# Diffusion backbone on one core: first eight modulation blocks in seven slots, sums of squares between them, x times the inverse ahead

## Chip, cores and metric

One core of one Trainium2 chip (trn2). The metric is device time in microseconds of one execution; a kernel's time is the median of its runs, and one further execution was profiled.

## The reference, cut to what matters

Two layers of a diffusion backbone act on 256 latent and 256 context tokens of width 1024. Every sub-layer is an RMSNorm, a shift and scale that come from a conditioning vector through one large matrix product per layer (the modulation), the sub-layer itself, and a gated addition. The change lies in the first norm of layer 0 and what stands around it.

```python
def rmsnorm(x, gain):
    xf = x.astype(jnp.float32)
    y = xf * lax.rsqrt(jnp.mean(xf * xf, axis=-1, keepdims=True) + EPS)
    return (y * gain.astype(jnp.float32)).astype(x.dtype)

def ada_mod(cond, w, b):
    m = jax.nn.silu(cond) @ w + b
    return jnp.split(m[..., None, :], 6, axis=-1)
...
        sh_m, sc_m, g_m, sh_f, sc_f, g_f = ada_mod(c, w_ada[layer], b_ada[layer])
        h = modulate(rmsnorm(x, norm_mix[layer]), sh_m, sc_m)      # h * (1 + scale) + shift
        y = even_mixer(h, w_in_even[j], ...)                       # begins with h @ w_in, 1024 x 1536
```

Behind it come the mixer, a dense SwiGLU, and in layer 1 a gated linear recurrence and top-2-of-8 experts, whose weights are most of the 480 MB that are read.

## The kernel before

**Precision.** Every large product is taken from fp32 in three passes of a high and a low part, both in fp32r (`three`, L633 to L638). The high part is made by ScalarE (L1533 for weights, L1583 for the first h), the low part by VectorE as the difference (L1919, L1975).

**Weights.** A projection's weights come in units of 128 x 1024 (512 KB), six raw slots (`raw`), each split into `w_hi` and `w_lo`; unit u waits for the split of unit u - 6 (`lo_done`). All loads are issued by SP in one order written out by hand (from L506 for modulation blocks, L469 for units), and a wait on SP holds everything that stands behind it.

**Modulation.** w_ada of a layer is taken in three thirds of 2048 columns, each in eight blocks of 128 rows (1 MB). Block a = 8t + kt belongs to third t. TensorE multiplies it with the conditioning vectors in `ada_unit` (L650, four fp32 matmuls of 512 columns, shown as eight instructions) and counts `ada_used`. There are three slots: two in the arena, one in `scratch`. The places in the arena for blocks 8 to 23 are columns 6144 and 8192. When eight blocks are done, ScalarE copies the row out (L1605), TensorE picks it into columns (`ada_pick`, L666), and VectorE adds the bias (`ada_cols`) and forms the coefficients.

**The beginning.** SP loads the small vectors, constants, x and ctx (each two tiles of 512 KB) and modulation blocks 0 to 2; blocks 3 to 7 each wait until their slot is used up. TensorE transposes x and ctx into eight tiles xT (L687), multiplies blocks 0 and 1, then makes eight sums of squares with a matrix of ones (`norm_sum`, L674), then blocks 2 to 7. The squares (L1550) alternate between two places, so each waits for the sum two ahead. VectorE scales the sum (L1960), ScalarE takes the Sqrt (L1577), VectorE the reciprocal (L1962). When the coefficients stand, `norm_dve` on VectorE takes, for each of the eight tiles, x times the inverse (L1985), two modulations of 256 columns (L1988), and the low part of the tile two back (L1975), with ScalarE's high part (L1583) between; four temporary tiles lie at arena columns 7680 to 9727, on the later places of modulation blocks. Therefore block 9 and 10 wait on SP for `h_done` 8 (L498).

**The first projection.** Its first two blocks of columns have four units each; a unit has 24 matmuls. Behind each unit stands one modulation block: blocks 8 to 11 in the first, 12 to 15 in the second. Ahead of block 8 SP issues the masks (448 KB), the DFT constants (640 KB), gmlp_w and gmlp_b (256 KB each), then block 8, unit 6, block 9, unit 7 and so on. GpSimd copies the masks once.

**Later.** The same pattern of units and modulation blocks goes on through layer 0. The expert weights run through a ring of 14 slots (L585), each freed by a split or by a use.

Of the kernel before, what the change touches and what calls it, by code (L numbers as in the profile page):

```python
# [34 lines left out]
D = 1024  # L35
# [23 lines left out]
R = 6  # L59
# [47 lines left out]
VEC_ROWS, B_ROWS = 12544, 12672  # L107
STATS = 13056
# [127 lines left out]
def build(nc, x, c, ctx_in, c_ctx, w_ada, b_ada, norm_mix, norm_ffn, norm_out, w_in_even, gmlp_wt, gmlp_b,  # L236
# [3 lines left out]
    with es:  # L240
# [3 lines left out]
        def sem(name):  # L244
            return es.enter_context(nc.semaphore(name))
# [50 lines left out]
        def ar(at, n):  # L296
            return arena[:, at:at + n]
# [27 lines left out]
        ada_in = [sem(f"ada_in{k}") for k in range(A_SLOTS)]  # L325
        ada_used, ada_half, ada_red = sem("ada_used"), sem("ada_half"), sem("ada_red")
# [60 lines left out]
        def ada_slot(a):  # L387

            at = A_SLOT_AT[a // KT]
            return scratch[:, :] if ada_place(a) == A_ACC else ar(at[ada_place(a)], A_COLS)  # L390
# [7 lines left out]
        def moe_seen(n):  # L398

            k = n % M_RING  # L400
            earlier = len(range(k, U_MOE, R)) if k < R else 0
            return moe_in[k], 16 * (earlier + n // M_RING + 1)
# [60 lines left out]
        def _(sp):  # L463
# [17 lines left out]
            def ada_load(a):  # L481

                t, kt = a // KT, a % KT
                last = max((b for b in range(a) if ada_place(b) == ada_place(a)), default=None)
                if a == 10:
                    sp.wait_ge(ada_used, 8)
                elif last is not None and last < A_PE:

                    sp.wait_ge(ada_used, last + 1)
                elif last is not None and ada_place(a) == A_ACC:  # L490

                    sp.wait_ge(ada_used, A_PE + 1)
# [12 lines left out]
                src = w_ada[t // 3][kt * P:(kt + 1) * P, t % 3 * A_COLS:(t % 3 + 1) * A_COLS]  # L505
                sp.dma_start(ada_slot(a), src).then_inc(ada_in[ada_place(a)], 16)  # L506
# [126 lines left out]
        def _(pe):  # L633
# [884 lines left out]
        def _(act):  # L1518
# [34 lines left out]
            def norm(n, width, layer, sh, streams):  # L1553


                act.wait_ge(coef_rdy, n)
# [18 lines left out]
            def norm_std(n, width):  # L1575
                act.wait_ge(var_done, n + 1)
                act.activation(ar(NORM_AT[n] + 2 * NT, width), ar(NORM_AT[n] + 2 * NT, width),  # L1577
                               ACT.Sqrt).then_inc(std_done, 1)

            def norm_hi(n, width):  # L1580
# [25 lines left out]
            norm_hi(0, NT)  # L1606
# [298 lines left out]
        def _(dve):  # L1905
# [50 lines left out]
            def norm_var(n, width):  # L1956

                inv = ar(NORM_AT[n] + 2 * NT, width)
                dve.wait_ge(sq_mm, KT * (n + 1))
                dve.tensor_scalar(inv, ps[:, 3, 0:width], 1.0 / D, EPS, ALU.mult, ALU.add).then_inc(var_done, 1)  # L1960
                dve.wait_ge(std_done, n + 1)
                link(dve.reciprocal(inv, inv))  # L1962

            def norm_dve(n, width, layer, gain, sh, sc, streams):

                base = NORM_AT[n]
                inv = ar(base + 2 * NT, width)
                for s in range(2):
                    m = dve.scalar_tensor_tensor(coef[:, :, s], adaT[:, layer, sc * KT:(sc + 1) * KT, s], 1.0,
                                                 vT[:, gain + layer * KT:gain + (layer + 1) * KT], ALU.add, ALU.mult)  # L1970
                link(m)

                def lo_h(kt):
                    dve.wait_ge(hhi_done, KT * n + kt + 1)
                    dve.tensor_tensor(hl(kt, 0, width), ar(base + (3 + kt % 4) * NT, width),  # L1975
                                      hh(kt, 0, width).bitcast(F32), ALU.subtract).then_inc(h_done, 1)

                for kt in range(KT):
                    if kt >= 2:
                        lo_h(kt - 2)  # L1980
                    if kt >= 4:

                        dve.wait_ge(h_done, KT * n + kt - 3)
                    t = ar(base + (3 + kt % 4) * NT, width)
                    link(dve.tensor_tensor(t, xT[:, kt, 0:width], inv, ALU.mult))  # L1985
                    for s in range(streams):
                        a, b = s * N_LAT, (s + 1) * N_LAT
                        m = dve.tensor_scalar(t[:, a:b], t[:, a:b], coef[:, kt, s:s + 1],  # L1988
                                              adaT[:, layer, sh * KT + kt, s:s + 1], ALU.mult, ALU.add)
                    m.then_inc(h32_done, 1)  # L1990
                    if n == 0 and kt in (6, 7):
                        split_to(split[0] + 1)
                lo_h(KT - 2)
                lo_h(KT - 1)

# [669 lines left out]
```

## Time and profile before

| | us |
|---|---|
| median of 3 runs | 1907.58 |
| lowest, highest | 1905.51, 1910.87 |
| the profiled execution: its own time | 1913.76 |
| its span, first to last instruction | 1911.9 |
| PE busy | 1767.9 (92%) |
| PEld busy | 1318.7 (69%) |
| DVE busy | 847.0 (44%) |
| ACT busy | 684.1 (36%) |
| chain that ended last | PE 69%, DMA 15%, DVE 7%, ACT 4%, SPq 3%, issue 2% |
| HBM read | 477.03 MB |
| mean granted TensorE clock | 0.966 |

PE is TensorE's matmul, PEld its weight load, DVE VectorE, ACT ScalarE, SP the engine whose queue issues the loads. The clock is a share of full speed, 2.4 GHz; the lower level is 0.50, 1.2 GHz. A matmul's end is modelled, so in a row of several the step from start to start is the better measure. An "idle before" in brackets names what ended it.

### The profile page before, as it was taken

The numbers are of one execution on the slowest core, as the hardware profiler recorded it, in microseconds if no ns is written. First come the engines' busy times: TensorE is split into PE (matmuls) and PEld (weight loads), VectorE is DVE, ScalarE is ACT, GpSimd is POOL, SyncE is SP. The second block draws the span as 40 slices with busy tenths as digits, with TensorE's granted clock in tenths as the row PEclk, the third lists the DMA queues.
The fourth block names the chain that finished last, engine by engine and source line by source line (L and its number), as shares of the span: only waits on it lengthen the run. The fifth ranks groups of instructions, "written<-read, shape, count | busy, mean of one in ns | idle before, by whom it ended". The sixth has DMA issues, their size and how long they took to land.

```text
span 1911.9 us, 28155 instructions
## 1 busy us (share of the span) xinstructions
PE 1767.9 (92%) x11488; PEld 1318.7 (69%) x11488; DVE 847.0 (44%) x1197; ACT 684.1 (36%) x893; POOL 3.5 (0%) x6
## 2 busy tenths in 40 slices
PE   5899899999998988997889999999998899998988
PEld 2567677888886978887777887766546777763434
DVE  2524424434533555656549965554104444520011
ACT  3222521222225535444358754443003444400001
POOL 0000000000000000000000000000000000000000
PEclk8899999999999999998979999999999899999998
DMA  8654166433631322120149979999999999999995
GB/s 324 246 186 154 34 231 231 172 103 138 225 98 46 100 89 77 60 84 23 67 166 322 377 297 407 409 409 409 408 409 385 340 359 381 401 409 409 409 409 238
DMA packets 161843, 479.96 MB, mean 251 GB/s; under 512 B 14976, under 2 KB 58160, under 8 KB 155568
## 3 DMA queue, kind: packets, MB, share of 16 engines
q1 hardware_dynamic: 161712, 478.14, 66.4%
q8 instruction: 91, 1.49, 0.3%
q14 instruction: 40, 0.33, 0.0%
HBM read 477.03 MB, written 1.05 MB: 250 GB/s over the span
## 4 chain that ended last, share of the span: by engine, by line
PE 69%; DMA 15%; DVE 7%; ACT 4%; SPq 3%; issue 2%; DVEq 0%; ACTq 0%
PE ps L636 15%; PE ps L638 15%; PE ps L637 15%; DMA arena<-in_moe_up 6%; DMA raw<-in_moe_up 5%; PE ps L1369 4%; DMA arena<-in_moe_w 3%; PE ps L1440 3%; SPq L585 2%; DVE w_lo L1919 2%; PE ps L1358 2%; PE ps L650 2%; PE ps L1432 1%; PE ps L1190 1%; ACT w_hi L1533 1%
## 5 line engine op out<-in xcount | busy, mean ns | idle before, releaser
L1919 DVE TENSOR_TENSOR w_lo<-raw,w_hi 128x1024 fp32r<-128x1024 f32 x242 | 292.5, 1221 | 367.8 <-ACT w_hi L1533 365.5
L1533 ACT ACTIVATE w_hi<-raw 128x1024 fp32r<-128x1024 f32 x242 | 252.5, 1056 | 463.2 <-PE ps L638 350.2
L636 PE MATMUL ps<-h_hi,w_hi 128*128 128x512 f32 (+1 forms) x736 | 284.2, 386 | 15.6 <-DVE h_lo L2013 10.8
L637 PE MATMUL ps<-h_hi,w_lo 128*128 128x512 f32 (+1 forms) x736 | 277.3, 377 | 0.0
L638 PE MATMUL ps<-h_lo,w_hi 128*128 128x512 f32 (+1 forms) x736 | 277.1, 376 | 0.0
L1919 DVE TENSOR_TENSOR w_lo<-arena,w_hi 128x1024 fp32r<-128x1024 f32 x144 | 172.0, 1220 | 123.8 <-ACT w_hi L1533 121.0
L1533 ACT ACTIVATE w_hi<-arena 128x1024 fp32r<-128x1024 f32 x144 | 151.4, 1059 | 160.4 <-DMA arena<-in_moe_up 92.0
L636 PEld LDWEIGHTS ps<-h_hi,w_hi 128*128 128x128 f32 x736 | 142.3, 193 | 59.6 <-issue 35.2
L638 PEld LDWEIGHTS ps<-h_lo,w_hi 128*128 128x128 f32 x736 | 141.6, 192 | 25.3
L637 PEld LDWEIGHTS ps<-h_hi,w_lo 128*128 128x128 f32 x736 | 142.2, 193 | 23.7 <-issue 0.5
L1369 PE MATMUL ps<-arena 128*64 128x256 f32 x1024 | 128.9, 387 | 9.5 <-DMA arena<-in_moe_up 7.8
L636 PE MATMUL ps<-w_hi,s_hi 128*128 128x512 f32 x336 | 134.8, 401 | 2.7 <-DVE s_lo L2442 2.4
L637 PE MATMUL ps<-w_hi,s_lo 128*128 128x512 f32 x336 | 131.6, 392 | 0.0
L638 PE MATMUL ps<-w_lo,s_hi 128*128 128x512 f32 x336 | 131.6, 392 | 0.0
L636 PE MATMUL ps<-w_hi,h_hi 128*128 128x512 f32 (+1 forms) x328 | 117.3, 358 | 0.0
L638 PE MATMUL ps<-w_lo,h_hi 128*128 128x512 f32 (+1 forms) x328 | 114.9, 350 | 0.0
L637 PE MATMUL ps<-w_hi,h_lo 128*128 128x512 f32 (+1 forms) x328 | 114.8, 350 | 0.0
L1369 PEld LDWEIGHTS ps<-arena 128*64 128x64 f32 x1024 | 66.7, 136 | 64.1 <-DMA arena<-in_moe_up 28.8
L1369 PE MATMUL ps<-raw,arena 128*64 128x256 f32 x768 | 94.1, 385 | 8.5 <-DMA raw<-in_moe_up 5.2
L636 PE MATMUL ps<-s_hi,w_hi 128*128 128x512 f32 (+1 forms) x240 | 90.5, 377 | 5.5 <-DVE s_lo L2286 5.5
L638 PE MATMUL ps<-s_lo,w_hi 128*128 128x512 f32 (+1 forms) x240 | 87.5, 365 | 0.0
L637 PE MATMUL ps<-s_hi,w_lo 128*128 128x512 f32 (+1 forms) x240 | 87.5, 365 | 0.0
(357 smaller groups left out, 2280.3 us busy)
## 6 DMA issues: line engine op xcount, KB each, us to landing
arena<-in_moe_up SPq DMA_DIRECT2D x256, 512.0 KB, 9.9
raw<-in_moe_up SPq DMA_DIRECT2D x192, 512.0 KB, 10.2
arena<-in_moe_w SPq DMA_DIRECT2D x128, 512.0 KB, 11.7
raw<-in_moe_w SPq DMA_DIRECT2D x96, 512.0 KB, 11.2
arena<-in_w_ada SPq DMA_DIRECT2D x36, 1024.0 KB, 5.1
raw<-in_ffn_w SPq DMA_DIRECT2D x66, 512.0 KB, 5.8
raw<-in_w_in_odd SPq DMA_DIRECT2D x40, 512.0 KB, 3.5
scratch<-in_w_ada SPq DMA_DIRECT2D x12, 1024.0 KB, 5.5
```

The lines of the kernel that those rows point to most:

```text
L585: sp.dma_start(moe_slot(n), src).then_inc(moe_in[n % M_RING], 16)
L636: pe.matmul(dst, s_h, m_h, start=start, stop=False, **kw)
L637: pe.matmul(dst, s_l, m_h, start=False, stop=False, **kw)
L638: return pe.matmul(dst, s_h, m_l, start=False, stop=stop, **kw)
L650: m = pe.matmul(ps[32 * j:32 * j + 32, bank, :], cond[:, a % KT, :], w[:, j * BANK:(j + 1) * BANK], start=start, stop=stop, skip_group_che ...
L1190: i = pe.matmul(ps[:, bank, kt * HALF:(kt + 1) * HALF], part[:, t * D + kt * P:t * D + (kt + 1) * P], onehot_s[:, t, 0:HALF], start=(q == ...
L1358: i = pe.matmul(ps[j * QUART:(j + 1) * QUART, 3, at:at + P], rows, src[:, kk * BANK + P * j:kk * BANK + P * (j + 1)], start=(kt == 0), sto ...
L1369: i = pe.matmul(ps[64 * j:64 * j + 64, bank, at:at + 256], ar(X_G + kt * HALF, HALF), src[:, kk * BANK + 256 * j:kk * BANK + 256 * j + 256 ...
L1432: i = pe.matmul(ps[j * QUART:(j + 1) * QUART, 7, 256 * q:256 * q + 256], rows, src[:, 256 * j:256 * j + 256], start=(kt == 0 and q == 0), ...
L1440: i = pe.matmul(ps[64 * j:64 * j + 64, 7 if both else 4, :], hidden_s[:, kt * HALF:(kt + 1) * HALF], src[:, j * BANK:(j + 1) * BANK], star ...
L1533: act.activation(w_hi[:, o % R, :], src, ACT.Copy).then_inc(hi_done, 1)
L1919: dve.tensor_tensor(w_lo[:, o % R, :], src, w_hi[:, o % R, :].bitcast(F32), ALU.subtract).then_inc(lo_done, 1)
```

## The change

Seven slots hold the first eight modulation blocks: block 0 at arena column 4096, block 1 at 10240, block 2 in `scratch`, block 3 in raw slots 2 and 3, block 4 in raw slots 4 and 5, block 5 at 6144, block 6 at 8192, and block 7 again at 4096, behind the use of block 0. Each has a semaphore of its own, lent by the expert ring. Units 2 to 5 of the projection wait until the raw slots are used. Blocks 8, 9 and 10 wait for `ada_used` 3, 6 and 7, and `h_done` no longer holds any of them. The masks wait for `ada_used` 8 in place of 7.

The squares go side by side to arena columns 0 to 4095, where the rows of x and ctx lay. A small Ln (`junk`) stands ahead of them. The eight sums stand behind modulation blocks 0 (two), 1 (two) and 2 (four). The inverse is made on ScalarE by Ln and Exp, in a place of its own. VectorE multiplies five tiles of x by the inverse as soon as it is there, and the other three between the modulations of tiles 0 to 2; each result takes the place of its square. The low part follows one tile behind its modulation in place of two. One weight unit, not two, is split before the row copy, and one more within the norm.

```diff
@@ places, semaphores
+FIRST_INV = 12288
+        first_in, x_inv = moe_in[R:], sem("x_inv")
@@ def ada_landed(a):
-            return ada_in[place], 16 * sum(ada_place(b) == place for b in range(a + 1))
+            if a < KT:
+                return first_in[a], 16
+            return ada_in[place], 16 * sum(ada_place(b) == place for b in range(KT, a + 1))
+
+        def first_slot(a):
+
+            if a in (3, 4):
+                return raw[:, 2 * a - 4:2 * a - 2, :].rearrange("p a c -> p (a c)")
+            return scratch[:, :] if a == 2 else ar((4096, 10240, None, None, None, 6144, 8192, 4096)[a], A_COLS)
+
+        def square_at(i):
+
+            return ar(X_ROWS + i * NT, NT)
@@ SP
-                if a == 10:
-                    sp.wait_ge(ada_used, 8)
+                if a < KT + A_SLOTS:
+
+                    if a >= KT - 1:
+                        sp.wait_ge(ada_used, (1, 3, 6, 7)[a - KT + 1])
...
-                if a in (9, 10):
-
-                    sp.wait_ge(h_done, KT)
...
-            for a in range(5):
+            for a in range(6):
                 ada_load(a)
             even_load(0)
+            for a in range(6, KT):
+                ada_load(a)
             even_load(1)
-            for a in range(5, KT):
-                ada_load(a)
             for u in range(2, R):
+
+                sp.wait_ge(ada_used, 4 if u < 4 else 5)
                 even_load(u)
-            sp.wait_ge(ada_used, 7)
+            sp.wait_ge(ada_used, 8)
             sp.dma_start(ar(MASK_F, C_MASK), msk).then_inc(mask_in, 16)
-            sp.wait_ge(ada_used, 8)
@@ TensorE
-            ada_unit(0, 1, True, False)
-            ada_unit(1, 1, False, False)
-            norm_sum(0, NT)
-            for a in range(2, KT):
-                ada_unit(a, 1, False, a == KT - 1)
+            def first_sum(i):
+
+                pe.wait_ge(sq_done, i + 1)
+                pe.matmul(ps[:, NORM_BANK[0], :], ones, square_at(i), start=(i == 0), stop=(i == KT - 1)).then_inc(sq_mm, 1)
+
+            for a in range(KT):
+                ada_unit(a, 1, a == 0, a == KT - 1)
+                for i in ((0, 1), (2, 3), (4, 5, 6, 7), (), (), (), (), ())[a]:
+                    first_sum(i)
@@ ScalarE
+            def first_hi():
+
                 for kt in range(KT):
-                    act.wait_ge(h32_done, KT * n + kt + 1)
-                    act.activation(hh(kt, 0, width), ar(NORM_AT[n] + (3 + kt % 4) * NT, width),
-                                   ACT.Copy).then_inc(hhi_done, 1)
-                    if n == 0 and kt in (4, 6):
+                    act.wait_ge(h32_done, kt + 1)
+                    act.activation(hh(kt), ar(X_ROWS + kt * NT, NT), ACT.Copy).then_inc(hhi_done, 1)
+                    if kt in (1, 4, 6):
                         split_to(split[0] + 1)
...
+            act.activation(junk[:, :], eps[:, :], ACT.Ln)
             for i in range(KT):
-                square(0, i, NT)
-            norm_std(0, NT)
-            split_to(2)
+                act.activation(square_at(i), xT[:, i, :], ACT.Square).then_inc(sq_done, 1)
+            act.wait_ge(sq_mm, KT)
+            inv = ar(FIRST_INV, NT)
+            act.activation(inv, ps[:, NORM_BANK[0], :], ACT.Ln, bias=eps[:, 0:1], scale=1.0 / D).then_inc(var_done, 1)
+            act.wait_ge(var_done, 1)
+            act.activation(inv, inv, ACT.Exp, scale=-0.5).then_inc(std_done, 1)
+            split_to(1)
@@ VectorE
+            def first_inv(kt):
+
+                dve.tensor_tensor(ar(X_ROWS + kt * NT, NT), xT[:, kt, :], ar(FIRST_INV, NT), ALU.mult).then_inc(x_inv, 1)
+
+            def first_norm():
+
                 def lo_h(kt):
+                    dve.wait_ge(hhi_done, kt + 1)
+                    dve.tensor_tensor(hl(kt), ar(X_ROWS + kt * NT, NT), hh(kt).bitcast(F32),
+                                      ALU.subtract).then_inc(h_done, 1)
+
+                dve.wait_ge(coef_rdy, 1)
                 for kt in range(KT):
+                    x = ar(X_ROWS + kt * NT, NT)
+                    dve.wait_ge(x_inv, kt + 1)
+                    for s in range(2):
+                        a, b = s * N_LAT, (s + 1) * N_LAT
+                        m = dve.tensor_scalar(x[:, a:b], x[:, a:b], coef[:, kt, s:s + 1],
+                                              adaT[:, 0, SH_M * KT + kt, s:s + 1], ALU.mult, ALU.add)
                     m.then_inc(h32_done, 1)
+                    if kt:
+                        lo_h(kt - 1)
+                    if kt < KT - 5:
+                        first_inv(kt + 5)
+                    if kt in (2, 6, 7):
                         split_to(split[0] + 1)
                 lo_h(KT - 1)
...
-            norm_var(0, NT)
-            split_to(2)
+            dve.wait_ge(std_done, 1)
+            for kt in range(5):
+                first_inv(kt)
+            split_to(1)
             ada_cols(0, 2)
             dve.wait_ge(ada_done, 1)
-            norm_dve(0, NT, 0, V_NMIX, SH_M, SC_M, 2)
+            norm_coef(0, V_NMIX, SC_M)
+            first_norm()
```

## Rows read from the trace of the kernel before

**Rows 1.** The chain that ended last, 0 to 75 us: start, duration, what.

```profile
31.05 9.55 DMA arena<-in_w_ada
...
42.64 0.60 ACT arena L1605
...
64.50 4.87 DMA arena<-in_w_ada
```

**Rows 2.** TensorE in order of time: start, us, engine, line, instruction, idle before.

```profile
18.90 1.92 PE L650 MATMUL ps<-arena,cond 128*32 128x512 f32 x16 [0.94 <-issue]
20.75 7.52 PE L674 MATMUL ps<-arena,con 128*128 128x512 f32 x16
28.20 1.07 PE L650 MATMUL ps<-scratch,cond 128*32 128x512 f32 x8
...
40.64 1.93 PE L650 MATMUL ps<-arena,cond 128*32 128x512 f32 x8 [0.59 <-DMA arena<-in_w_ada]
43.29 1.88 PE L666 MATMUL ps<-con,arena 128*128 128x8 f32 x8 [0.72 <-ACT arena L1605]
49.84 0.77 PE L636 MATMUL ps<-h_hi,w_hi 128*128 128x512 f32 x1 [4.67 <-DVE h_lo L1975]
...
58.20 0.50 PE L636 MATMUL ps<-h_hi,w_hi 128*128 128x512 f32 x1
...
69.41 1.94 PE L650 MATMUL ps<-arena,cond 128*32 128x512 f32 x8 [5.47 <-DMA arena<-in_w_ada]
...
79.22 0.50 PE L636 MATMUL ps<-h_hi,w_hi 128*128 128x512 f32 x1
...
85.89 0.50 PE L636 MATMUL ps<-h_hi,w_hi 128*128 128x512 f32 x1
```

**Rows 3.** The DMA queue's own waits, 49 to 90 us: total, times, longest.

```profile
SPq L498 <- DVE h_lo L1975: 19.6, 1, 19.6
```

**Rows 4.** ScalarE in order of time, near the start.

```profile
18.83 1.15 ACT L1550 ACTIVATE arena<-xT 128x512 f32<-128x512 f32 x2
```

**Rows 5.** ScalarE in order of time, the later norm with Ln and Exp.

```profile
204.69 1.28 ACT L1636 ACT_TABLE_LOAD   x1
205.98 0.20 ACT L1636 ACTIVATE junk<-eps 128x1 f32<-128x1 f32 x1
...
224.44 1.28 ACT L1567 ACT_TABLE_LOAD   x1
225.73 0.63 ACT L1567 ACTIVATE arena<-arena 128x512 f32<-128x512 f32 x1
```

**Rows 6.** VectorE in order of time, beginning.

```profile
33.16 2.36 DVE L1919 TENSOR_TENSOR w_lo<-raw,w_hi 128x1024 fp32r<-128x1024 f32 x2
...
45.77 0.69 DVE L1985 TENSOR_TENSOR arena<-xT,arena 128x512 f32<-128x512 f32 x1
46.50 0.73 DVE L1988 TENSOR_SCALAR arena<-arena,coef,adaT 128x256 f32<-128x256 f32 x2
...
49.02 0.68 DVE L1975 TENSOR_TENSOR h_lo<-arena,h_hi 128x512 fp32r<-128x512 f32 x1
```

**Rows 7.** Stretches: busy of PE, PEld, DVE, ACT, POOL; PEclk, DMA share, GB/s.

```profile
10.00:19.00 9.00, 5.42 (x36) 5.22 (x40) 0.95 (x5) 4.73 (x10) 0.00 (x0) 1.00 1.01 422
32.00:40.00 8.00, 3.81 (x16) 0.40 (x16) 3.49 (x3) 0.00 (x0) 0.00 (x0) 0.57 1.00 397
38.90:52.80 13.90, 7.92 (x31) 4.39 (x24) 7.38 (x18) 2.49 (x4) 1.48 (x1) 0.50 1.01 376
66.00:68.00 2.00, 0.00 (x0) 0.00 (x0) 1.82 (x2) 0.00 (x0) 0.00 (x0) 0.79 0.80 319
75.00:140.00 65.00, 65.00 (x319) 44.69 (x317) 14.53 (x17) 14.03 (x17) 0.00 (x0) 1.00 0.65 234
800.00:1000.00 200.00, 166.93 (x1106) 154.04 (x1106) 113.37 (x223) 91.20 (x134) 1.80 (x1) 0.90 0.23 80
```

**Rows 8.** The SP queue in order of time: start, us, line, transfer issued.

```profile
1256.31 9.68 SPq L585 DMA_DIRECT2D arena<-in_moe_w  x8
```

More of the change, by code:

```diff
@@ L384, in ada_landed @@
             place = ada_place(a)
-            return ada_in[place], 16 * sum(ada_place(b) == place for b in range(a + 1))
+            if a < KT:
[7 more added lines that the diff above has]
+            return ar(X_ROWS + i * NT, NT)
         def ada_slot(a):
+            if a < KT:
+                return first_slot(a)
             at = A_SLOT_AT[a // KT]
@@ L400, in moe_seen @@
             k = n % M_RING
-            earlier = len(range(k, U_MOE, R)) if k < R else 0
+            earlier = len(range(k, U_MOE, R)) if k < R else 1
             return moe_in[k], 16 * (earlier + n // M_RING + 1)
@@ L505, in ada_load @@
                 src = w_ada[t // 3][kt * P:(kt + 1) * P, t % 3 * A_COLS:(t % 3 + 1) * A_COLS]
-                sp.dma_start(ada_slot(a), src).then_inc(ada_in[ada_place(a)], 16)
+                sp.dma_start(ada_slot(a), src).then_inc(first_in[a] if a < KT else ada_in[ada_place(a)], 16)
             vr = ar(VEC_ROWS, P)
@@ L1553, in norm @@
             def norm(n, width, layer, sh, streams):
-                act.wait_ge(coef_rdy, n)
+                act.wait_ge(coef_rdy, n + 1)
                 for i, kt in enumerate(NORM_ORDER[n]):
@@ L1573, in norm @@
                     m.then_inc(hhi_done, 1)
[L1575 to L1580, printed above, removed]
+            def first_hi():
                 for kt in range(KT):
-                    act.wait_ge(h32_done, KT * n + kt + 1)
-                    act.activation(hh(kt, 0, width), ar(NORM_AT[n] + (3 + kt % 4) * NT, width),
-                                   ACT.Copy).then_inc(hhi_done, 1)
-                    if n == 0 and kt in (4, 6):
+                    act.wait_ge(h32_done, kt + 1)
+                    act.activation(hh(kt), ar(X_ROWS + kt * NT, NT), ACT.Copy).then_inc(hhi_done, 1)
+                    if kt in (1, 4, 6):
                         split_to(split[0] + 1)
@@ L1599, in _ @@
             act.wait_ge(x_out, 8)
+            act.activation(junk[:, :], eps[:, :], ACT.Ln)
             for i in range(KT):
-                square(0, i, NT)
-            norm_std(0, NT)
-            split_to(2)
+                act.activation(square_at(i), xT[:, i, :], ACT.Square).then_inc(sq_done, 1)
[5 more added lines that the diff above has]
+            split_to(1)
             act.wait_ge(ada_used, KT)
             act.activation(ar(ADA_ROW, BANK), ps[:, 1, :], ACT.Copy).then_inc(ada_row, 1)
-            norm_hi(0, NT)
+            first_hi()
             split_to(U_IN_EVEN + 4 + LEAD)
@@ L1954, in ada_cols @@
                 m.then_inc(ada_done, 1)
[L1956 to L1971, printed above, removed]
+            def first_inv(kt):
+                dve.tensor_tensor(ar(X_ROWS + kt * NT, NT), xT[:, kt, :], ar(FIRST_INV, NT), ALU.mult).then_inc(x_inv, 1)
@@ L1973, in lo_h @@
+            def first_norm():
                 def lo_h(kt):
-                    dve.wait_ge(hhi_done, KT * n + kt + 1)
-                    dve.tensor_tensor(hl(kt, 0, width), ar(base + (3 + kt % 4) * NT, width),
-                                      hh(kt, 0, width).bitcast(F32), ALU.subtract).then_inc(h_done, 1)
+                    dve.wait_ge(hhi_done, kt + 1)
+                    dve.tensor_tensor(hl(kt), ar(X_ROWS + kt * NT, NT), hh(kt).bitcast(F32),
+                                      ALU.subtract).then_inc(h_done, 1)
+                dve.wait_ge(coef_rdy, 1)
@@ L1978, in norm_dve @@
                 for kt in range(KT):
[L1979 to L1986, printed above, removed]
+                    x = ar(X_ROWS + kt * NT, NT)
+                    dve.wait_ge(x_inv, kt + 1)
+                    for s in range(2):
@@ L1987, in norm_dve @@
                         a, b = s * N_LAT, (s + 1) * N_LAT
-                        m = dve.tensor_scalar(t[:, a:b], t[:, a:b], coef[:, kt, s:s + 1],
-                                              adaT[:, layer, sh * KT + kt, s:s + 1], ALU.mult, ALU.add)
+                        m = dve.tensor_scalar(x[:, a:b], x[:, a:b], coef[:, kt, s:s + 1],
+                                              adaT[:, 0, SH_M * KT + kt, s:s + 1], ALU.mult, ALU.add)
                     m.then_inc(h32_done, 1)
-                    if n == 0 and kt in (6, 7):
+                    if kt:
+                        lo_h(kt - 1)
@@ L1992, in norm_dve @@
+                    if kt < KT - 5:
+                        first_inv(kt + 5)
+                    if kt in (2, 6, 7):
                         split_to(split[0] + 1)
-                lo_h(KT - 2)
                 lo_h(KT - 1)
```

## The prediction

> **What bounds the kernel now.** I read the chain that ended last first, cut to the beginning. It leaves the engines twice for the same kind of load [rows 1]: 9.55 us up to 40.64, for the eighth block of modulation weights, and 4.87 us from 64.50, for the tenth (block 9; I count from 0). TensorE's list in order of time shows what surrounds them [rows 2]. Blocks 0 and 1 are multiplied from 18.90, then eight sums of squares take 20.75 to 28.20, then come blocks 2 to 4; only then does the slot of block 4 come free, and blocks 5, 6 and 7 are waited for one by one, the last until 40.64. After that the pick starts at 43.29, the first projection matmul at 49.84, its second unit at 58.20; block 9 is waited for 5.47 us and starts at 69.41; the fourth unit starts at 79.22 and the next at 85.89. The load of block 9 was itself held on SP for 19.6 us by h_done, the eighth low part of h [rows 3], because its slot was the norm's temporary room. From 75 to 140 TensorE is busy 65.00 of 65.00 us at a granted clock of 1.00 [rows 7]. So the end of the kernel hangs on when the fourth unit of the first projection starts (79.22), and I price the change by that instant.
>
> **Where later time is decided.** Behind 79.22 every load and every split waits for an event that moves with the computation (lo_done, pe_used, h_done), the expert stream too, so I carry a shift there one to one to the end. The load order behind block 10 is unchanged.
>
> **Part 1, the first eight blocks.** SP now issues blocks 0 to 6 with no wait; only block 7 waits, for block 0's use at about 20, long before its turn. Before, everything issued early (inputs, blocks 0 to 2) was down at about 19.0. Behind it lie now blocks 3 to 7, 5 x 1.049 = 5.24 MB, and projection unit 0 (0.52 MB): 5.77 MB. The rate was 422 GB/s in 10 to 19 and 397 in 32 to 40 [rows 7]: 13.7 or 14.5 us, data complete at 32.7 to 33.5. Bytes and arrivals of blocks 5 to 7 before show the semaphore 0.9 to 1.8 us behind the data; I take block 7 landed at 34.7 (33.6 to 35.3).
>
> **Part 2, the sums behind the blocks.** The squares now stand side by side, so ScalarE needn't wait for TensorE between them, but a junk Ln goes ahead: x_out complete at 18.83 [rows 4], table load 1.28 and the junk's step 0.11 (the instruction lasts 0.20) [rows 5], the first square 20.2 to 20.9, each further one 0.52 (two took 1.15 [rows 4]). TensorE: block 0 from 18.90 takes 0.93 (two took 1.85 up to 20.75), then idles to 20.95. Then seven blocks and eight sums, 0.93 each at full clock (eight sums in 7.45 [rows 2]), would end at 20.95 + 15 x 0.93 = 34.9, and block 7 could start at 34.0. The data is later by 0.7: block 7 runs 34.7 to 35.7. Before, it ended at 42.6. The clock: TensorE has no pause over 1.2 us up to there, and before it was granted 1.00 until about 33.1 (0.57 over 32 to 40 is full for 1.1 us of 8 [rows 7]), after it had stopped at 31.0. So block 7 and the pick run at full clock: the pick 0.99 in place of 1.88 [rows 2] (its cost halves with a doubled clock). Bounds: half clock at both costs 1.8; a block 7 at 33.6 gives 0.8.
>
> **Part 3, the inverse.** The last sum ends at 30.3; Ln 0.65, a table load 1.28, Exp 0.63 [rows 5]: inverse ready at 33.0. VectorE: five products at 0.61 to 36.1, one weight split of 1.18 [rows 6] to 37.3. They replace a Sqrt with its table and a reciprocal of 3.35, all off the path before and after. The row copy is 35.7 to 36.4 (0.60 [rows 1]), the pick 36.4 to 37.4, so VectorE is free in the same tenth. Then the column adds and coefficients, 0.6 from the pick's end to 45.77 before: the norm starts at 38.0.
>
> **Part 4, the first tile.** Before, from 45.77: product, modulation, product, modulation, and only at 49.02 the first low part; TensorE at 49.84, 4.07 later. Now: modulation 0.73, product of tile 5 0.61, modulation 0.73, low part 0.68 [rows 6], 2.8 with the handover. TensorE starts at **40.8 against 49.84: 9.0 us earlier**. VectorE's pace is 1.95 a tile for tiles 0 to 2, with two splits slipped in, against TensorE's 2.7 a tile (24 matmuls of a unit in 5.7), so no tile is waited for. ScalarE takes split 1 between high parts 1 and 2; it ends at about 41.7, before the modulation of tile 2. I cost this at nothing; if the cover went, a split is 1.06 on ScalarE and 1.18 on VectorE.
>
> **Part 5, block 9.** Its load waits for ada_used 6 alone, its slot free since 34. SP's order from 31 on: units 1 to 5, the mask (behind ada_used 8), three constants, block 8, unit 6, block 9. From block 7's data (33.1) to block 8's these are 2.62 + 1.64 + 1.05 = 5.31 MB, at 376 GB/s [rows 7] 14.1 us: data at 47.2, landed 48.1 to 49.0. Unit 0 of the projection began at half clock before and lasted with block 8 8.36 (49.84 to 58.20 [rows 2]); TensorE pauses 37.4 to 40.8 now, and the clock had fallen 2.1 and 3.2 us after it stopped (33.1, and 67.2 by 0.79 over 66 to 68 [rows 7]), so I keep 8.36. Block 8 is wanted at 48.2: a wait of 0 to 0.8, I take 0.2. Block 9 lands at about 53, wanted at 55.0: no wait. So: 40.8 + 8.4 + 0.2 = 49.4 for the second unit, two steps of unit plus block at 6.67 (79.22 to 85.89 [rows 2]) put the fourth unit at 62.7. Before 79.22: **16.5 us saved**, 9.0 ahead of the first matmul and 7.5 in the wait for block 9 with the half clock after it. SP's issue takes longer where transfers are outstanding, eight of 512 KB in 9.68 us [rows 8], their own transfer time; with eight megabytes queued at the start SP may be held, but behind full DMA engines.
>
> **A rule of the skill against it.** Each of the two switches ahead of the inverse showed 1.28, and Exp began at 225.73, 0.01 behind its load [rows 5]: no more than the load is lost. The Trainium skill, ScalarE: Activation LUTs, section What ACT_TABLE_LOAD costs, adds a drain of 1380 ns to each switch. By it the squares would come 1.4 later, TensorE's sums end at 36.3 and the saving be 15.9. The same page, section Table sets: the hidden batching unit, says that Ln and Exp share one load; the trace disagrees (a load at 224.44 between the two), and by the page nothing would change, since VectorE isn't last by more than a tenth.
>
> **Rivals.** (a) The data is late: the deeper queue spreads its lag over all early transfers, block 7 lands at 36 to 37 and block 8 makes TensorE wait 1 to 2 us in the first projection. For: the lag doubled from 0.9 to 1.8 as more lay behind a block. Against: 422 GB/s with 5 MB queued. 1.8 + 1.5 off: 13.2 saved, 1894.4. (b) Only one of the two halves arrives: the change doesn't shorten the wait for block 9 because another holds its load (SP's in-order queue, one wait ahead of it on h or lo_done). Every wait ahead of it in the new order is met by 36, which speaks against. 16.5 - 7.5 = 9.0: 1898.6. (c) The clock doesn't fall in the shorter pause of 3.4 us, or falls just ahead of its end and returns sooner: 1.7 more, but block 8 then takes 1 back; 17.5 to 18.2, 1889.7. (d) Slower: the granted clock of the later stages. It was 0.90 over 800 to 1000 [rows 7], in which TensorE pauses for VectorE; shifted in time, such pauses may fall the other way. Each us of busy time moved to half clock costs 0.5. It decides only once 2 x (16.5 + 5.7) = 44 us more of busy time run at half; the stretch 800 to 1000 has 40 now (0.10 x 2 x 200). With 48: 1907.6 - 16.5 + 24 = 1915. Nothing in the trace makes it go one way. (e) Same: half of that, with (a).
>
> **The numbers.** The sum is against the profiled execution, 1913.76 (span 1911.9): 1897.3. That one stood 6.2 above the median of the three runs, 1907.58, so I predict 1907.6 - 16.5 = **1891.1**. Chances: forecast 0.60, (a) 0.14, (b) 0.06, (c) 0.13, (d) 0.03, (e) 0.04. No change is within 0.3% (5.7 us), about what a measurement of this kernel can tell: faster 0.93, same 0.04, slower 0.03. The forecast alone spans 1888 to 1894 by its bounds and the runs' own spread of 2.7 up and 2.1 down; the range takes in (a) and (c) and most of (b): 1885.5 to 1898.5.
>
> **What would show it.** The inverse's Exp at about 33 with its table load ahead; block 7's matmuls of 1.0, not 1.9, at about 34.7; pick at 36.4; first projection matmul at 40.8; no wait over 1 us for a modulation block behind it; fourth unit at 62.7; 75 to 140 busy throughout; every later landmark 16.5 earlier. Wrong would be a wait for scratch (block 8) over 2 us, block 7 after 36.5, or a shift at the fourth unit that the end of the span doesn't show.

## The result and the profile after

| us | before | after |
|---|---|---|
| median (20 runs each) | 1910.33 | 1899.24 |
| lowest, highest | 1905.51, 1914.12 | 1893.94, 1907.63 |
| the profiled execution, its own time | 1913.76 | 1907.63 |
| its span | 1911.9 | 1905.8 |
| mean granted clock | 0.966 | 0.963 |

The ratio is 0.9948, interval 0.9937 to 0.9960: about 0.5% faster, 11.1 us by the medians and 9.4 by the means, clear of the spread. I had said 1891.1 (16.5 less), range 1885.5 to 1898.5; the median lies 0.7 outside it. Of the 8.1 us between forecast and result 2.7 are the base (I had counted from the 1907.58 of three runs, and twenty gave 1910.33), and 5.4 are the saving. The new kernel's runs spread more than the old one's: 13 of 20 lie at 1893.9 to 1900.4 (mean 1897.5), 7 at 1903.9 to 1907.6 (mean 1905.8), none between. The profiled execution is the slowest of them.

**The beginning is as forecast.** First the chain that ended last, after, cut to the beginning (start, us, what); it answers to [rows 1].

```profile
17.91 0.94 issue
18.85 1.10 PE ps L666 x8
19.97 15.03 DMA arena<-in_w_ada
35.04 1.11 PE ps L666 x8
36.17 0.61 ACT arena L1625
36.82 1.07 PE ps L682 x8
37.92 0.27 DVE adaT L1973 x2
38.49 0.73 DVE arena L1993 x2
39.23 0.60 DVE arena L1978
39.82 0.65 DVE arena L1993 x2
40.47 0.61 DVE h_lo L1984
41.22 0.76 PE ps L652
```

Only one wait for a modulation block is left, block 7's, and the sums are off the chain. TensorE in order of time, after, against [rows 2]:

```profile
18.85 1.07 PE L666 MATMUL ps<-arena,cond 128*32 128x512 f32 x8 [0.94 <-issue]
20.84 1.98 PE L713 MATMUL ps<-arena,con 128*128 128x512 f32 x4 [0.92 <-ACT arena L1617]
22.75 1.06 PE L666 MATMUL ps<-arena,cond 128*32 128x512 f32 x8
23.75 1.98 PE L713 MATMUL ps<-arena,con 128*128 128x512 f32 x4
25.66 1.06 PE L666 MATMUL ps<-scratch,cond 128*32 128x512 f32 x8
26.66 3.70 PE L713 MATMUL ps<-arena,con 128*128 128x512 f32 x8
...
35.04 1.07 PE L666 MATMUL ps<-arena,cond 128*32 128x512 f32 x8 [1.11 <-DMA arena<-in_w_ada]
36.82 1.06 PE L682 MATMUL ps<-con,arena 128*128 128x8 f32 x8 [0.72 <-ACT arena L1625]
41.22 0.76 PE L652 MATMUL ps<-h_hi,w_hi 128*128 128x512 f32 x1 [3.34 <-DVE h_lo L1984]
...
50.35 0.50 PE L652 MATMUL ps<-h_hi,w_hi 128*128 128x512 f32 x1
...
63.68 0.50 PE L652 MATMUL ps<-h_hi,w_hi 128*128 128x512 f32 x1
```

Block 7 and the pick take 1.07 and 1.06, full clock, where they took 1.93 and 1.88. The fourth unit of the projection starts at 63.68 against 79.22: 15.5 us earlier, 1.0 less than the 16.5 forecast. The Gelu's table load on ScalarE, behind eight units, shows the same, 90.59 against 106.14. I use it as a landmark from here on: "beginning" is what lies ahead of it, "late part" what lies behind, which is the same program in all kernels but one (c3).

**The late part is not.** It took 1911.9 - 106.1 = 1805.8 us before and 1905.8 - 90.6 = 1815.2 after. Set side by side, instruction by instruction at the times of the changed kernel, the two lists of TensorE keep their distance of 15 to 16 us up to 880, and then lose it in steps of 0.8 to 3 us that lie in stretches of half clock: 12 are left at 1000, 8 at 1105, 7 at 1300. Some comes back in between (8.4 at 1400); 6 are left at the end. That is the last sign of being wrong that I had named: a shift at the fourth unit that the end of the span doesn't show.

### The profile page after: what moved, and what is told of

It is laid out like the page before. It is cut to its first block, busy times and chain, and to the rows that moved or that the text cites. A ratio compares the mean times of both kernels' runs of the same rounds, so it can differ in the third digit from the quotient of the medians.

```text
span 1905.8 us, 28154 instructions
## 1 busy us (share of the span) xinstructions
PE 1774.0 (93%) x11488; PEld 1328.4 (70%) x11488; DVE 842.7 (44%) x1195; ACT 685.8 (36%) x896; POOL 4.5 (0%) x6
## 4 chain that ended last, share of the span: by engine, by line
PE 71%; DMA 12%; DVE 6%; ACT 4%; SPq 3%; issue 3%; DVEq 0%; ACTq 0%
PE ps L652 16%; PE ps L653 15%; PE ps L654 15%; DMA arena<-in_moe_up 6%; PE ps L1389 5%; DMA arena<-in_moe_w 3%; PE ps L1460 3%; SPq L601 3%; DVE w_lo L1939 2%; PE ps L1378 2%; DMA raw<-in_moe_up 2%; PE ps L1452 1%; PE ps L666 1%; PE ps L1210 1%; ACT w_hi L1553 1%
```

## What the experiments were to settle

A spell is a stretch in which the granted clock is 0.50. The forecasts set theories against each other:

- P: the shift passes to the end, the rest is chance.
- C: the half-clock spells of the later stages fall otherwise behind the new beginning.
- R (second and third set of runs): the late part's loss to half clock is chance in each execution.
- S (second set): the late part is shorter where it starts later.
- G (third set): the loss is set by where the late part stands against the instants at which the clock changes.

"Lost" below is TensorE's busy time times one minus the granted clock, summed over windows of 1 us behind the landmark. All times are medians; the number of executions stands behind.

**The changed kernel once more (a1).**

> The changed kernel once more, for a second profile. Both theories expect its beginning as in the first profile: first projection matmul at 41.2 us, second group of columns at 70.35. Theory P (what is saved ahead of 70.35 passes to the end, the rest was chance): the part behind 70.35, 1835.4 us in the first profile, comes near the 1826.0 that the kernel before had behind its same landmark (85.89); about 1826 to 1830. Theory C (the half-clock spells of the recurrent and expert stages are another set after this beginning): it stays above 1828, and the difference to 1826.0 is in us of TensorE busy at half clock, of which I count 41 behind 75 us before and 54 after.

Measured 1897.86 (6), ratio 0.9931 (0.9914 to 0.9948). Its profiled execution took 1890.77, 17 us less than the first one of the same kernel. Stretches of the first profile of the changed kernel, the whole late part ahead, then a place in the recurrent stage, one in the expert stage (columns as in [rows 7]):

```profile
90.60:1905.80 1815.20, 1702.54 (x11142) 1283.66 (x11141) 808.32 (x1133) 651.15 (x847) 1.80 (x1) 0.96 0.66 248
650.00:670.00 20.00, 13.38 (x49) 10.60 (x48) 13.97 (x22) 12.16 (x17) 0.00 (x0) 0.74 0.32 98
1085.00:1105.00 20.00, 20.00 (x108) 17.71 (x107) 9.87 (x9) 9.05 (x9) 0.00 (x0) 0.83 0.58 206
1285.00:1295.00 10.00, 10.00 (x55) 8.45 (x52) 4.72 (x4) 4.26 (x5) 0.00 (x0) 0.83 1.03 409
```

The same of a1:

```profile
90.80:1888.90 1798.10, 1688.40 (x11142) 1270.27 (x11141) 807.99 (x1133) 650.97 (x847) 1.80 (x1) 0.97 0.66 250
650.00:670.00 20.00, 13.39 (x59) 10.91 (x58) 14.45 (x22) 12.68 (x18) 0.00 (x0) 0.83 0.30 91
1085.00:1105.00 20.00, 20.00 (x100) 16.91 (x100) 14.61 (x13) 13.35 (x13) 0.00 (x0) 1.00 0.75 268
1285.00:1295.00 10.00, 10.00 (x45) 6.10 (x44) 4.69 (x4) 4.52 (x5) 0.00 (x0) 1.00 1.03 409
```

The same 11142 matmuls kept TensorE busy 14.1 us longer in the one than in the other, VectorE and ScalarE 0.3 and 0.2; the clock is the only column that explains it. Near 1090 and 1290 TensorE has no pause at all, and yet one execution has half clock there and the other none. Behind the second group of columns a1 took some 1818 us: P's 1826 to 1830 and C's over 1828 are both missed, on the lower side. That two executions of one kernel could lie 17 us apart neither had foreseen; that the difference is busy time at half clock is C's.

**Block 9 held by the norm again (a2).** SP waits for the eighth low part ahead of blocks 9 and 10.

```diff
+                if a in (9, 10):
+                    sp.wait_ge(h_done, KT)
```

> Blocks 9 and 10 wait for h_done 8 again. Both: block 9 is issued when the last low part is done (about 54.5) and lands near 59.5; TensorE waits about 3.5 us and goes on at half clock, so the second group of columns starts 5.5 to 7.5 later than 70.35. Theory P: the end is 5.5 to 7.5 later than the changed kernel's median (about 1905 to 1906 where that is 1899.2). Theory C: anything from 0 to 12 later, since the late part need not be the same.

Measured 1902.45 (6), ratio 0.9963 (0.9946 to 0.9980), 4.6 above a1. Block 9 in its trace:

```profile
60.52 1.93 PE L669 MATMUL ps<-arena,cond 128*32 128x512 f32 x8 [3.97 <-DMA arena<-in_w_ada]
```

The landmark moved to 98.00, 7.4 later, as the prediction's step for block 9 has it (7.5). The median gave 4.6 against a1 and 3.2 against the twenty runs: P's 5.5 to 7.5 is missed, and C's 0 to 12 would have fitted almost any result.

**Four matmuls more (a3).** Ahead of the second group of columns, on TensorE at full clock. I had priced them at 0.93 each, 3.7 together; from the block ahead to the block behind, the trace has 10.10 us where the changed kernel has 6.67, so they added 3.4.

```diff
             for blk, bank in ((0, 0), (1, 4)):
+                for _ in range(4 if blk == 1 else 0):
+                    pe.matmul(ps[:, 5, :], ones, con[:, 0:BANK], start=True, stop=True)
                 for k in range(4):
```

> Four fp32 matmuls of 512 columns (0.93 us each) on TensorE ahead of the second group of columns, at full clock: that group starts 3.7 later, at 74.1, nothing else changes. Theory P: the median is 3.7 later than that of the changed kernel. Theory C: the late part depends on when it begins, so the median differs from plus 3.7 by over 2, in either direction.

Measured 1898.36 (6), 0.5 above a1, by means 3.9 above. Landmark 93.97, 3.4 later than the first profile's. P's 3.7 isn't seen in the median, and two of six runs lie at 1905.7 and 1909.8: with six runs of such a spread neither figure is firm.

**Three matmuls in the first pause (a4).** The same matmul three times, behind the pick.

> Three fp32 matmuls of 512 columns on TensorE in its pause ahead of the first projection (37.9 to 41.2), so that the clock need not fall there. Both: projection starts at 41.2, its first unit at full clock (5.7, not 8.1): second group of columns at about 67.8 to 68.0, by 2.5 earlier. Theory P: median 2.5 below that of the changed kernel. Theory C: the late part changes as well, the median by anything from minus 8 to plus 3.

Measured 1898.90 (6). The landmark came at 92.15, not 2.5 earlier but 1.5 later, so both theories' beginning was wrong here, and the median settles nothing between them. TensorE at full clock runs into block 8:

```profile
41.34 0.47 PE L652 MATMUL ps<-h_hi,w_hi 128*128 128x512 f32 x1 [0.66 <-DVE h_lo L1985]
...
49.28 1.07 PE L666 MATMUL ps<-scratch,cond 128*32 128x512 f32 x8 [2.22 <-DMA scratch<-in_w_ada]
```

Block 8 lands at 49.3. In the changed kernel's first profile no wait shows, since there the first unit, part of it at half clock, ends at 49.3 as well. Behind the wait of 2.22 us the clock fell after all (columns as in [rows 7]):

```profile
50.80:54.20 3.40, 3.40 (x9) 2.63 (x9) 3.40 (x6) 2.59 (x4) 0.00 (x0) 0.50 1.04 414
```

That is 1.7 us of work lost, and the landmark is late by about as much.

**The kernel before once more (b1).**

> The kernel before once more, for a second profile. Both theories expect its beginning as in the first: the Gelu table load at 106.1 us. Theory R (the late part is the same program with the same time on average, and varies from execution to execution by how much of TensorE's busy time falls to half clock): the part behind 106.1 is 1764 plus that busy time, 1798 to 1815 us, as in the four profiles of kernels with the new beginning (1760 plus it). Theory S (the late part is steadier and shorter behind the old beginning): it comes within 3 us of the first profile's 1805.8, and the 5 timed runs spread over less than 7 us.

Measured 1911.92 (11), ratio 1.0008 (0.9997 to 1.0018). The landmark came at 107.47, 1.3 later than in the first profile; the late part took 1803.9 and lost 41.5. Both theories fit that; the eleven runs spread 7.4 where the twenty of the new beginning spread 13.7, which speaks for S or for something that only the new beginning has.

**All sums behind block 1 (b2).**

```diff
-                for i in ((0, 1), (2, 3), (4, 5, 6, 7), (), (), (), (), ())[a]:
+                for i in ((), (0, 1, 2, 3, 4, 5, 6, 7), (), (), (), (), (), ())[a]:
```

> All eight sums of squares behind modulation block 1, as before the change, not two, two and four behind blocks 0, 1 and 2. TensorE fills its pause of 0.9 us at 19.9 with block 1 and is done with block 6 about 1 us earlier; the Exp comes about 1.9 us earlier (30.5), but block 7 is still not landed before 34.9 to 35.1. Both theories: first projection matmul within 0.5 us of 41.2 and the median within 3 us of the changed kernel's. If it is over 3 us later, the interleaving was worth something.

Measured 1903.57 (6), 4.3 above the changed kernel. By the rule that I had set this would make the interleaving worth something, but the trace says no: block 7 is waited for as before, and the landmark is at 90.42.

```profile
35.08 1.07 PE L666 MATMUL ps<-arena,cond 128*32 128x512 f32 x8 [1.37 <-DMA arena<-in_w_ada]
36.87 1.06 PE L682 MATMUL ps<-con,arena 128*128 128x8 f32 x8 [0.72 <-ACT arena L1625]
```

Four of the six runs lie above 1903.5. The median of six was the wrong yardstick; a landmark is the right one.

**Constants behind block 9, with the first pause filled (b3).** The mask and the three constants move in SP's order; the three matmuls are a4's.

```diff
-            sp.wait_ge(ada_used, 8)
-            sp.dma_start(ar(MASK_F, C_MASK), msk).then_inc(mask_in, 16)
...
             for i in range(2 * KT):
                 ada_load(KT + i)
                 if R + i < U_FFN:
                     even_load(R + i)
+                if i == 1:
+                    sp.wait_ge(ada_used, 8)
+                    sp.dma_start(ar(MASK_F, C_MASK), msk).then_inc(mask_in, 16)
...
```

> Masks and the three constants (1.64 MB) are issued behind block 9 and unit 7 instead of ahead of block 8, and three fp32 matmuls fill TensorE's pause ahead of the first projection as in the run with three matmuls there, where TensorE then waited 2.22 us for block 8. Both: block 8 lands at about 45.5, no wait for it; unit 0 at full clock from 41.3 to 47.0; the Gelu table load at 87.9 to 88.2 (90.6 in the changed kernel, 92.15 with the fill alone). Theory P: median 2.5 below the changed kernel's. Theory R: the same on average, within the late part's own spread of some 8 us either way.

Measured 1895.36 (5), ratio 0.9915 (0.9902 to 0.9928), landmark 88.45 where 87.9 to 88.2 was forecast. Better than both kernels: the landmark is 2.1 ahead of the changed kernel's and 3.7 ahead of a4's, which has the same three matmuls with the constants in their old place. Block 8 starts at 47.21 with no wait. Moving the constants alone was not run.

**Eight matmuls more (b4).** As a3, with eight. They were priced at 7.5 and added 6.9 in the trace.

> Eight fp32 matmuls of 512 columns (0.93 us each) ahead of the second group of columns: the Gelu table load at 98.1. The kernel with four of them started that late part 3.4 later than the changed kernel and ended only 0.5 later by medians. Theory R: 7.4 later than the changed kernel's median, within 3. Theory S: the late part gets shorter where it starts later, so that the median is 3 to 5 later only (1901 to 1903).

Measured 1901.79 (5), ratio 0.9951 (0.9938 to 0.9963), all five between 1900.5 and 1903.7. Landmark 96.66 where 98.1 was forecast (0.6 of that is the added time, the rest an earlier end of the first half-clock spell, 44.7 against 46.5), late part 1803.3, lost 43.0. S expected this median: 6.9 us of added busy time cost 3.9 against a1 and 2.6 against the twenty runs, and R's 7.4, within 3, is missed. But S's reason doesn't hold: a1 starts its late part 5.9 earlier and has the shorter one (1798.1). The small spread, 3.2, was foreseen by neither.

**What orders them.** In each profile, the changes of the granted clock stand on instants with one fixed spacing, the same in all fourteen: each of the 40 to 50 changes of a profile lies within 0.001 us of them. Against the start of the kernel these instants lie anywhere, from execution to execution (at fractions of 0.11 to 0.97 of the spacing). I took the place of the landmark between two of them, as a fraction of the spacing (how far behind the landmark the next instant is):

| profile | landmark | fraction | late part | lost | late - lost |
|---|---|---|---|---|---|
| a1 after | 90.78 | 0.22 | 1798.1 | 38.1 | 1760.0 |
| before | 106.14 | 0.58 | 1805.8 | 41.3 | 1764.4 |
| c2 before + 3.4 | 108.09 | 0.73 | 1803.8 | 39.1 | 1764.7 |
| c4 none ahead | 90.13 | 0.79 | 1802.4 | 42.6 | 1759.8 |
| b4 after + 6.9 | 96.66 | 0.79 | 1803.3 | 43.0 | 1760.3 |
| b1 before | 107.47 | 0.80 | 1803.9 | 41.5 | 1762.5 |
| a2 hold 9 | 98.00 | 0.84 | 1811.3 | 50.1 | 1761.2 |
| c3 pauses filled | 88.04 | 0.86 | 1811.4 | 50.2 | 1761.2 |
| a3 after + 3.4 | 93.97 | 0.86 | 1814.0 | 54.3 | 1759.7 |
| a4 fill | 92.15 | 0.89 | 1814.8 | 56.3 | 1758.5 |
| c1 before + 2.2 | 107.73 | 0.99 | 1814.1 | 54.2 | 1759.8 |
| b2 sums | 90.42 | 0.02 | 1815.2 | 57.1 | 1758.0 |
| b3 constants | 88.45 | 0.06 | 1811.0 | 47.4 | 1763.6 |
| after | 90.59 | 0.08 | 1815.2 | 54.1 | 1761.1 |

Two things stand in it. The late part less its lost time is 1758 to 1765 in all fourteen. And from 0.22 to 0.80 the loss is 38 to 43 us, from 0.84 over 0 to 0.08 it is 47 to 57. I call these the good and the bad side. On the bad side more is lost from 560 to 660 us behind the landmark (6.0 to 6.2 against 3.1 to 3.4) and from 690 to 830 (6.9 to 7.1 against 5.1 to 5.2; c3, whose late part is another program, has 4.2 and 8.1). And all eight profiles of the bad side have spells in the expert stage about 1000 and 1198 us behind the landmark that all six of the good side lack. The bounds of the sides were drawn after the first ten rows; the sides of c1 and c2 were foretold from these.

**The kernel before with five short matmuls more (c1), and with four long ones (c2).** c1 has five matmuls of 256 columns, c2 four of 512, at a3's place. By the forecast the first should carry it to the bad side, the second nearly once around. Between the blocks on either side, the traces show 2.2 and 3.4 added.

```diff
+                for _ in range(5 if blk == 1 else 0):
+                    pe.matmul(ps[:, 5, 0:256], ones, con[:, 0:256], start=True, stop=True)
```

> The kernel before with five fp32 matmuls of 256 columns (2.33 us together) on TensorE ahead of the second group of columns. Theory G (the clock changes only at instants of the chip's own; in six profiles the late part lost 47 to 57 us to half clock and in four 38 to 43, and which it is depends on where the late part stands against these instants; the beginning of the kernel before, with its two long half-clock spells, always put it on the good side): 2.33 us move it to the bad side in most executions. The late part is 8 to 12 longer, the profile shows half-clock spells near 1110 and 1308, and the median is 8 to 14 above that of the kernel before. Theory R (chance alone): the median is 2.3 above, within 1.5.

> The kernel before with four fp32 matmuls of 512 columns (3.73 us together) at the same place. Theory G: that much brings the late part back to nearly the old standing against the chip's instants, so the good side again: median 3 to 5 above that of the kernel before, thus 4 or more below the kernel with only 2.33 us added. Theory R: 3.7 above, and 1.4 above the kernel with 2.33 added.

Measured: c1 1917.23 (12), ratio 1.0024 (1.0006 to 1.0041), from 1907.9 to 1923.9: eight runs at 1916.3 to 1923.9, of which seven at a mean clock of 0.959 to 0.961, four at 1907.9 to 1912.4 and 0.966 to 0.969. c2 1915.87 (6), ratio 1.0028 (1.0016 to 1.0040), from 1913.7 to 1919.2. So 2.2 us cost 6.2 and 3.4 us cost 4.8, and the former spread 16 us where the latter spread 5.5. G had expected 8 to 14 and at least 4 between the two; the median fell short of both, and four of twelve executions were as fast as those of the good side. R's 2.3, within 1.5, is missed as well, and so is R's 1.4 more for c2, which came out 1.4 less. But the intervals of the two runs overlap, so the medians alone don't decide. The profiles are clearer. First c1, then c2, the expert stage at the two places:

```profile
1100.00:1120.00 20.00, 20.00 (x108) 17.70 (x107) 9.87 (x9) 9.11 (x10) 0.00 (x0) 0.83 0.58 204
1303.00:1313.00 10.00, 10.00 (x54) 8.82 (x54) 4.52 (x5) 4.37 (x6) 0.00 (x0) 0.83 1.03 408
```

```profile
1100.00:1120.00 20.00, 20.00 (x118) 17.61 (x118) 12.68 (x12) 11.57 (x12) 0.00 (x0) 1.00 0.69 254
1303.00:1313.00 10.00, 10.00 (x45) 6.09 (x44) 4.81 (x4) 4.61 (x5) 0.00 (x0) 1.00 1.02 409
```

**Two later pauses filled (c3).** b3, and five fp32 matmuls of 512 columns on `con` into bank 0, ahead of the h waits of the norm at 205 and of the one at 595.

> The kernel with the constants behind block 9 and three matmuls in the first pause, and besides five fp32 matmuls of 512 columns (4.7 us) in each of the two later norms' pauses of 5.4 us (near 205 and 595), into a bank that is free there. Both theories: no half-clock spell at 208 and 597, where four profiles of the new beginning lost 3.0 to 3.9 us of busy time and those of the old 4.8 and 5.4. Late part as 1760 plus its lost busy time: by 3.4 less on average, median 1891 to 1893 where the constants behind block 9 gave 1895.4, spread 8 or more since the good and the bad side both still occur.

Measured 1893.79 (6), ratio 0.9902 (0.9886 to 0.9918), from 1887.6 to 1901.2: the lowest median of all. The two spells are gone, and TensorE's wait of 5.39 us ahead of the first is 1.10. First b3, then c3:

```profile
200.00:215.00 15.00, 9.61 (x29) 6.05 (x28) 7.33 (x17) 9.29 (x18) 0.00 (x0) 0.77 0.00 1
590.00:610.00 20.00, 14.61 (x51) 10.26 (x50) 12.83 (x28) 13.52 (x27) 0.00 (x0) 0.83 0.00 1
```

```profile
200.00:215.00 15.00, 13.90 (x47) 8.13 (x45) 7.33 (x17) 9.72 (x19) 0.00 (x0) 1.00 0.00 1
590.00:610.00 20.00, 18.90 (x68) 12.01 (x67) 14.18 (x28) 14.11 (x27) 0.00 (x0) 1.00 0.00 1
```

It is 1.6 below b3 where 3.4 were expected; with spreads of 7 and 14 us the difference isn't shown by these runs. Its profile was on the bad side.

**No products ahead (c4).** Each product stands ahead of its tile's modulation.

> The changed kernel with no product of x and the inverse ahead: each stands directly ahead of its tile's modulation. Both theories: the first low part comes behind product, modulation, product, modulation, low part: 0.6 later than with the change's order, first projection matmul at 41.8 instead of 41.2; the block 8 wait and the rest of the beginning as in the changed kernel, so the Gelu table load at 90.9 to 91.2. The five products ahead are worth 0.3 to 0.6.

Measured 1897.44 (two runs only), level with the changed kernel. The first projection matmul came at 41.70, 0.5 later, as expected, but the landmark at 90.13, no later: the first unit of that execution came back to full clock at 45.0, of the changed kernel's first profile at 46.5. So the products ahead gained 0.5 at the first matmul; what of that reaches the landmark at an equal clock, one profile can't tell.

## Why the prediction was wrong, point by point

- **Part 1, block 7.** Right: landed at 35.0 (34.7 forecast), its matmuls at full clock.
- **Part 2, the sums.** Right in time: Ln starts behind the last at 30.4 (30.3). That they stand between the blocks is worth nothing (b2), because the data of block 7 is later anyway; what the seven slots give is that data.
- **Part 3, the inverse.** Exp from 32.4 to 33.0, with its own load; norm from 38.5 (38.0 forecast). Each switch of tables cost the 1.28 of its load: junk ran at 20.07 and the first square at 20.17, behind a load that began at 18.77. Ln ended at 31.09, its load ran from 31.10, Exp started at 32.40. So nothing of the drain that the Trainium skill (ScalarE: Activation LUTs, What ACT_TABLE_LOAD costs) adds was seen, and Ln and Exp had a load between them here as well.
- **Part 4, the first tile.** 41.22 against 40.8 forecast, 8.6 earlier than before instead of 9.0. TensorE's pace was put at 2.7 a tile; half of a unit's 5.7 is 2.85, which changes nothing in the sum.
- **Part 5, block 9.** Right: no wait. Restoring it (a2) moved the landmark 7.4. The first unit with block 8 took 9.1 (41.22 to 50.35) where 8.36 and a wait of 0.2 were forecast: its half clock lasted 5.3 us, up to 46.5, against 3.7 before (49.84 to 53.5). With the 0.4 of part 4 this is the 1.0 by which the fourth unit came late. Block 8 just hid, and became the bound once the first unit ran at full clock (a4); rival (c) had priced that wait at 1, it was 2.2.
- **The step that failed** is the one headed "where later time is decided": "so I carry a shift there one to one to the end". It put the change of the late part at nothing. The late part without its lost time did stay the same (1758 to 1765 us in fourteen profiles), but TensorE's clock didn't move with the computation: with it the late part took 1798 to 1815, and by the means below 5.9 us more behind the new beginning than behind the old.
- **Rival (d)** had the mechanism and was misused. I asked only whether the clock could turn the gain into a loss, which takes 44 us of busy time, and let it stand at 0.03. A part of such a loss could have come with any of the other outcomes, and neither the forecast's own span (1888 to 1894) nor the full range had room for it.

The sum with what was measured: the beginning of the kernel before ended at 106.1, 107.5, and less the time added 105.6 and 104.7 in c1 and c2, on average 106.0. That of the changed kernel ended at 90.6 and 90.8, 90.7. Saved: 15.3. A run's own time is 1.85 above its span, so the means of 20 runs (1909.8 and 1900.4) leave 1802.0 for the late part before and 1807.8 after: 5.9 longer by the unrounded figures, and 15.3 - 5.9 = 9.4, which is the difference of the means by construction. The split is no firmer than the landmarks, which lie 2.8 apart before; with the two unchanged profiles alone it is 16.1 and 6.7. Of the 5.9, 7 of 20 runs on what I take for the bad side, 8.3 above the others, make 2.9. That these seven are bad-side executions is argued from their times and their mean clocks (0.963 to 0.966 against 0.967 to 0.972), not shown by traces, but for the profiled one.

The mean clocks of the runs give the late part's loss a second way. The span times one minus the mean clock averages 63.9 us over 18 runs of the kernel before and 61.8 over 20 after. The beginnings lose 12 to 14 of it before (half of their 24 to 27 us of half clock; in c2 8.5) and 3.4 after, which leaves 50 to 55 and 58. In the two first profiles 0.78 to 0.79 of such a loss fell on time in which TensorE was busy. So I estimate that the late part lost 2 to 6 us more busy time after, 4.7 with the average of the four beginnings: most of the 5.9 is lost clock by this count, on whichever side the runs stood.

**Why the old beginning avoided the bad side.** Its landmark moved with the instants: over four profiles (b1, the first, c1, c2) it moved by 2.8 us, while the fractions, with the added time taken off again, stayed at 0.58 to 0.80. Its last half-clock spell, 6.8 us in all four, ended between 73.0 and 76.1, and the landmark followed 31.4 to 32.1 later each time. (The spell ahead of it took 20.5 us in two of them, 17.1 in c1, and was split in c2.) TensorE's work resumes its speed only at the end of the spell, so a later instant ends the beginning later. The changed kernel's beginning has one spell of 6.8 us, and its landmark moved little: 90.1 to 90.8 over four profiles (c4, b2 and its own two), while that spell ended anywhere from 45.0 to 47.1 and the fraction went from 0.79 over 0.02 and 0.08 to 0.22. If its fractions are spread evenly, the bad side, 0.24 to 0.42 of the round, should take a quarter to two fifths of its runs; 7 of 20 look so. This fits all fourteen profiles, but I tried no kernel that keeps the old spells with the new loads.

**What stays open.** The 3.0 us that remain of the 5.9: even the faster thirteen runs (mean 1897.5) leave 1805 for the late part against 1802. And why the expert stage at 1090, where TensorE has no pause, loses its clock on one side only. In the first profile of the changed kernel the clock fell at 1091.0, within a row of 32 matmuls of 64 columns (1088.5 to 1093.3) that follows 32 of 128, and again at 1289.0, at the end of such a row:

```profile
1085.00:1091.00 6.00, 6.00 (x56) 5.99 (x54) 3.67 (x3) 2.08 (x2) 0.00 (x0) 1.00 0.97 366
1091.00:1098.00 7.00, 7.00 (x24) 5.97 (x24) 0.85 (x2) 1.65 (x2) 0.00 (x0) 0.51 0.22 90
```

a1 has the same rows and kept its clock at 1.00 through them. No run varies these matmuls, so that they are the cause isn't shown.

## What to carry to other kernels

Forecast the shift at a landmark right behind the change, and price the rest apart: where later stages have pauses, a shift of 15 us lost over a third on the way to the end, while the late part without its lost clock time stayed within 7 us. Judge an edit of a few us by such a landmark in the trace and not by the median of six runs, when one kernel's executions lie 17 us apart. Before a load is moved ahead, look at what hides the next one: block 8 was bound as soon as the first unit ran at full clock, and with 1.6 MB of constants moved behind it, that pause filled, the landmark came 2.1 earlier (b3).

## What the hardware showed unexpectedly

TensorE's clock can fall to half in a stretch in which it never waits: 0.83 over 1085 to 1105 with 20.00 us busy of 20.00. The same kernel on the same data took 1890.8 and 1907.6 us, and 14.1 us of the 17 are in TensorE's busy time alone. Adding 2.2 us of work to the kernel before cost 6.2 us by the median, adding 3.4 us cost 4.8; the intervals of the two overlap. And a run of matmuls put into a pause kept the clock: with five of them ahead of each of the two later norms, it was granted 1.00 where it had been 0.77 and 0.83 (c3).
